# Expert groups: the one-hot block as stationary operand, four transposes after it, and the next one-hot block formed before the fourth expert's copy

## What is computed

```python
def hierarchical_moe(xn, w_group, w_router, w_gate, w_up, w_down):
    xt = xn.reshape(T, D)                                  # 256 x 1024, f32
    group_p = softmax(xt @ w_group)                        # 8 groups
    group_w, group_id = lax.top_k(group_p, 1)              # one group a token
    in_group = ...                                         # its 4 experts' logits
    top_logits, local_id = lax.top_k(in_group, 2)          # two of the four
    gates = group_w * softmax(top_logits)
    ...
    def expert_block(args):
        xb, e = args
        h = silu(xb @ w_gate[e]) * (xb @ w_up[e])          # 1024 -> 256
        return h @ w_down[e]                               # 256 -> 1024
    ...                                                    # y = sum of gate * expert output
```

## Time and profile before

| | us |
|---|---|
| median of 3 runs | 2758.59 |
| lowest, highest | 2754.98, 2763.64 |
| the profiled execution | 2754.4 |
| its span in the profile | 2752.6 |

### The profile page before, as it was taken

The page is one execution under the profiler, slowest core; times in us unless marked ns, Lnnn a source line. Parts: engine busy times, 40 slices in busy tenths (PEclk is TensorE's granted clock), DMA queues, the critical chain, the costliest instruction groups (busy, mean ns, idle before and its releaser), DMA issues. The chain is left out here.

```text
span 2752.6 us, 27889 instructions
## 1 busy us (share of the span) xinstructions
PE 2201.7 (80%) x8660; PEld 1182.1 (43%) x8660; DVE 1349.2 (49%) x2884; ACT 771.5 (28%) x2246; POOL 1050.1 (38%) x1107
## 2 busy tenths in 40 slices
PE   4778886766877878878877767769789998889997
PEld 2455552322333343434533222226555555655554
DVE  5656567865467466465664754441522223332222
ACT  1324232332434333353342333332410002410001
POOL 4015556667666546555566666650000000000000
PEclk9788988888998989989998988889889999978998
DMA  9548889999999999989999999992069994218995
GB/s 362 205 147 337 313 308 408 350 377 406 408 413 410 404 353 387 364 312 364 348 337 358 407 376 366 373 350 93 21 239 412 405 408 149 77 66 353 391 406 218
DMA packets 236993, 879.67 MB, mean 320 GB/s; under 512 B 23282, under 2 KB 29954, under 8 KB 214338
## 3 DMA queue, kind: packets, MB, share of 16 engines
q0 software_dynamic: 149488, 543.97, 51.6%
q1 hardware_dynamic: 87380, 334.23, 30.9%
HBM read 877.07 MB, written 1.05 MB: 319 GB/s over the span
## 5 line engine op out<-in xcount | busy, mean ns | idle before, releaser
L1481 PE MATMUL PS<-arena 128*128 128x512 f32 x2048 | 1032.4, 655 | 355.6 <-issue 197.1
L2117 DVE CUSTOM_DVE_ANT_0 JK<-arena,PS 128x1024 bf16<-128x1024 f32 x512 | 625.1, 1221 | 418.9 <-DMA arena<-in_peer_u_dram,IDX 293.1
L1481 PEld LDWEIGHTS PS<-arena 128*128 128x128 f32 x2048 | 407.3, 208 | 939.6 <-issue 889.9
L892 POOL DMA_INDIRECT arena<-in_peer_v_dram,IDX x512 | 500.2, 977 | 462.9 <-PE PS L1481 248.8
L889 POOL DMA_INDIRECT arena<-in_peer_u_dram,IDX x512 | 504.6, 986 | 334.7 <-DVE IDX L2090 162.7
L1031 ACT ACTIVATE ACTV<-DOT 128x1 f32<-128x1 f32 x512 | 102.0, 199 | 755.4 <-DVE DOT L2117 496.9
L1831 PE MATMUL PS<-arena,HT 128*64 128x256 f32 x2048 | 238.0, 385 | 0.0
L1044 ACT ACTIVATE arena<-IDENT,GACT 128x128 f32<-128x128 f32 x512 | 205.5, 401 | 91.3 <-remote 63.1
L1831 PEld LDWEIGHTS PS<-arena,HT 128*64 128x64 f32 x2048 | 142.6, 138 | 85.6 <-issue 21.4
L1039 ACT ACTIVATE GACT<-ACTV,GATE 128x1 f32<-128x1 f32 x512 | 150.8, 295 | 21.6 <-issue 3.5
L1459 PE MATMUL PS<-HT,arena 128*128 128x128 f32 x896 | 125.3, 304 | 35.3 <-issue 33.9
(11 more groups left out here) (339 smaller groups left out, 1863.8 us busy)
## 6 DMA issues: line engine op xcount, KB each, us to landing
arena<-in_w_gate_dram SPq DMA_DIRECT2D x64, 1024.0 KB, 9.5
arena<-in_w_up_dram SPq DMA_DIRECT2D x64, 1024.0 KB, 11.5
arena<-in_w_down_dram SPq DMA_DIRECT2D x64, 1024.0 KB, 8.2
arena<-in_w_ada_dram SPq DMA_DIRECT2D x24, 2048.0 KB, 12.3
arena<-in_w_in_dram SPq DMA_DIRECT2D x11, 2048.0 KB, 14.7
arena<-in_peer_wq_dram SPq DMA_DIRECT2D x10, 2048.0 KB, 8.1
arena<-in_w_out_dram SPq DMA_DIRECT2D x6, 2048.0 KB, 8.5
arena<-in_peer_u_dram,IDX POOLq DMA_INDIRECT x512
```

The source lines that it names most:

```text
L892: pool.indirect_dma_start(out=GV[b], out_offset=None, in_=v_rows, in_offset=off).then_inc(v_loaded[b], 16)
L1481: last = pe.matmul(PO[:, half, :], DIAG[:, n % DIAGS, :], GV[BUF[n]][:, half * 512:(half + 1) * 512], start=(j == 0), stop=False, skip_gro ...
L2117: dve.tensor_tensor_reduce(JUNK, GU[BUF[n]], HP[tt].rearrange("p b n -> p (b n)"), 1.0, 0.0, ALU.mult, ALU.add, DOT[:, s:s + 1]).then_inc( ...
```

## The change

`pick` swaps its operands. For each token tile and each half of the width, SEL's 64 slot columns (128x64) are stationary and 512 columns of HR move; the halves go to PSUM partitions 0 to 63 and 64 to 127 of bank 0. That is 4 matmuls in place of 16, and the result is not turned. ACT copies bank 0 (128x512) to a new buffer XS. A new step `turn_picked` transposes XS in four blocks of 128 columns into bank 1, and ACT copies that (128x512) to HTB, whose layout is now (m, c, t) with slice k = 4c + m. The semaphores rows_turned and rows_turned_out carry the two new hand-overs; picked and picked_out count one for each group, not two.

On PE turn_picked stands behind down of the group before and ahead of turn; slot_gates moves from behind the first gate and up to ahead of it, except in a layer's first group. On DVE, select of the next group stands ahead of the wait for the fourth expert's gate and up and of its copy, no longer behind them.

```diff
-        HTB = HTF[:, 0:KT * BT].rearrange("p (k t) -> p k t", k=KT)
+        HTB = HTF[:, 0:KT * BT].rearrange("p (m c t) -> p m c t", c=2, t=BT)
...
+        XS = mod[:, 9752:10264]
...
 # ACT, body, s == 0
-                        for c in range(2):
-                            act.wait_ge(picked, 2 * i + (2 * l * NGB + c + 1))
-                            act.activation(HTB[:, c * 4:(c + 1) * 4].rearrange("p k t -> p (k t)"), PS[:, c, 0:4 * BT],
-                                           ACT.Copy).then_inc(picked_out, 1)
+                        act.wait_ge(picked, i + (l * NGB + 1))
+                        act.activation(XS, PS[:, 0, :], ACT.Copy).then_inc(picked_out, 1)
+                        act.wait_ge(rows_turned, i + (l * NGB + 1))
+                        act.activation(HTB.rearrange("p m c t -> p (m c t)"), PS[:, 1, :], ACT.Copy).then_inc(rows_turned_out, 1)
...
 # PE
-                    for k in range(KT):
-                        for tt in range(TT):
-                            last = pe.matmul(PS[:, k // 4, (k % 4) * BT:(k % 4 + 1) * BT], HR[:, tt, k * P:(k + 1) * P],
-                                             SEL[:, tt, 0:BT], start=(tt == 0), stop=(tt == 1))
-                        if k % 4 == 3:
-                            last.then_inc(picked, 1)
+                    for tt in range(TT):
+                        for c in range(2):
+                            last = pe.matmul(PS[c * BT:(c + 1) * BT, 0, :], SEL[:, tt, 0:BT],
+                                             HR[:, tt, c * 512:(c + 1) * 512], start=(tt == 0), stop=(tt == 1))
+                    last.then_inc(picked, 1)
+
+                def turn_picked(i):
+                    pe.wait_ge(picked_out, i + (l * NGB + 1))
+                    for m in range(4):
+                        last = pe.transpose(PS[:, 1, m * P:(m + 1) * P], XS[:, m * P:(m + 1) * P], IDENT)
+                    last.then_inc(rows_turned, 1)
...
+                    if s == 0:
+                        turn_picked(i)
                     if n:
                         turn(*before(i, s, 1))
+                    if s == 0 and n:
+                        slot_gates(i)
...
+                    if s == 0:
+                        pe.wait_ge(rows_turned_out, i + (l * NGB + 1))
                     for k in range(KT):
-                        if s == 0 and k % 4 == 0:
-                            pe.wait_ge(picked_out, 2 * i + (2 * l * NGB + k // 4 + 1))
...
-                    if s == 0:
+                    if s == 0 and not n:
                         slot_gates(i)
...
 # DVE, body
-                    dve.wait_ge(gate_up_done, b + 1)
-                    if s == 0:
-                        dve.wait_ge(slot_gates_out, i + (l * NGB + 1))
-                    dve.tensor_scalar(GUO[:, s % 2], PS[:, 2 + s % 2, 0:DE], GS[:, s:s + 1], None,
-                                      ALU.mult).then_inc(gate_up_out, 1)
                     if s == EXP_RING - 1:
                         if n == EXP_RING:
                             dve.wait_ge(added, 2 * TT * i + 2 * TT * l * NGB)
                         dve.wait_ge(sel_turned, i + (l * NGB + 1))
                         dve.wait_ge(sel_step, i + (l * (NGB + 1) + 1))
                         select(i + 1)
+                    dve.wait_ge(gate_up_done, b + 1)
+                    if s == 0:
+                        dve.wait_ge(slot_gates_out, i + (l * NGB + 1))
+                    dve.tensor_scalar(GUO[:, s % 2], PS[:, 2 + s % 2, 0:DE], GS[:, s:s + 1], None,
+                                      ALU.mult).then_inc(gate_up_out, 1)
```

More of the change, by code:

```diff
@@ L583, in build @@
         gates_placed = sem("gates_placed")
+        rows_turned = sem("rows_turned")
+        rows_turned_out = sem("rows_turned_out")
         slot_gates_done = sem("slot_gates_done")
@@ L1296, in body @@
                         act.activation(SELT.rearrange("p t q -> p (t q)"), PS[:, 5, 0:TT * P], ACT.Copy).then_inc(sel_turned_out, 1)
-                blocks(act, l, body, silu, [(picked_out, *groups(l, 2)), (silu_done, *passes(l)),
+                blocks(act, l, body, silu, [(picked_out, *groups(l)), (rows_turned_out, *groups(l)), (silu_done, *passes(l)),
                                             (slot_gates_out, *groups(l)), (sel_turned_out, *groups(l))])
@@ L1826, in body @@
                         pe.wait_ge(expert_loaded[s], i * 48 + (l * NBX // EXP_RING + 1) * 48)
+                    if s == 0:
+                        pe.wait_ge(rows_turned_out, i + (l * NGB + 1))
                     for k in range(KT):
-                        if s == 0 and k % 4 == 0:
-                            pe.wait_ge(picked_out, 2 * i + (2 * l * NGB + k // 4 + 1))
                         for c, w in enumerate((WG[s], WU[s])):
-                            last = pe.matmul(PS[c * BT:(c + 1) * BT, 2 + s % 2, 0:DE], HTB[:, k, :],
+                            last = pe.matmul(PS[c * BT:(c + 1) * BT, 2 + s % 2, 0:DE], HTB[:, k % 4, k // 4, :],
                                              w[:, k, :], start=(k == 0), stop=(k == KT - 1))
                     last.then_inc(gate_up_done, 1)
-                    if s == 0:
+                    if s == 0 and not n:
                         slot_gates(i)
@@ L1842, in flush @@
                         spread_rows(i, tt, 2 * tt)
-                blocks(pe, l, body, flush, [(picked, *groups(l, 2)), (gate_up_done, *passes(l)), (turned, *passes(l)),
+                blocks(pe, l, body, flush, [(picked, *groups(l)), (rows_turned, *groups(l)), (gate_up_done, *passes(l)), (turned, *passes(l)),
                                             (down_done, *passes(l)), (slot_gates_done, *groups(l)),
```

## The result

| | us |
|---|---|
| before, median of 12 runs | 2767.24 (2754.92 to 2778.34) |
| changed, median of 12 runs | 2740.22 (2729.81 to 2756.17) |
| ratio, 95% interval | 0.9905 (0.9878 to 0.9931) |
| changed, profiled execution and its span | 2742.74, 2741.0 |

The change makes the kernel 27 us faster, 19 to 34 by the interval. The forecast was 34.6 us off a median of 2758.59, so 2724, with a range of 2713 to 2740: the direction is right, the gain four fifths of the forecast, and the time 0.2 us above the range. Three things were off. One decides the gain: a term of the sum, the spare time of the weights' loads.

What follows compares the result with a forecast made beforehand. PE was taken to bound the expert loops, with the DMA queue 0.69 us per group behind. Gains of 13.6 (layer 0), 14.1 (layer 1) and 6.4 us (clock drops), 34 in all, gave 2724 us, range 2713 to 2740.

Steps and rivals of the forecast that it cites:

- Select, 1.05: Between two groups, DVE's earlier select hides behind gate and up, so PE's wait before pick goes: 1.05 us gained per handover.
- Pick, 1.84: Pick as 4 wide matmuls of down's shape takes 1.87 us in place of 3.71: 1.84 us gained per handover.
- Four transposes, 0.87: The new transposes of the picked rows on PE cost 0.87 us per handover, between 0.74 and 1.04.
- Second copy, 0 with up to 0.3 kept: ACT's copy after the transposes hides behind turn and slot_gates: cost 0, with 0.3 us kept for the range.
- Sum of a handover, 2.0: Select plus pick minus transposes: 2.0 us gained per handover, range 1.6 to 2.3; 28.3 us over both layers.
- First group, 0: A layer's first group, without cover and mostly at 1.2 GHz: new pick, copies and transposes 6.98 us against 6.99, gain 0.
- Drops of the clock: Layer 1's two groups of 33.99 us, slowed by clock drops inside pick, return to normal: 6.4 us gained.
- Spare time of the loads: Weight loads have 5 to 10 us of spare, likeliest 8 to 10, while the queue falls behind 1.3 us per group.
- Loads bind early: Rival: loads bind from the first group, only the queue's dry moments, 9.7 us, are gained: 2743 to 2749 us; chance 0.08.
- Drops stay: Rival: the clock drops stay, two of them at other places, so 28 us are gained: 2731 us; chance 0.13.
- Halves apart: Rival: the new pick's two halves don't run side by side, a handover gains 0.4 us: 2747 us; chance 0.04.
- slower: Rival: six transposes and slot_gates in a row pull the clock down at every handover, 10 us slower: 2769 us; chance 0.04.

Runs made afterwards that it cites:

- split wait: Changed kernel with a semaphore of its own for down's weights, so gate and up waits only for its own two transfers: median 2611.16 us, ratio to before 0.9858.
- select_late: Changed kernel with select put back behind the fourth expert's copy, the new pick kept: loops 238.1 and 238.6 us, ratio to before 0.9898.
- select_early: Kernel before with only select moved ahead of the fourth expert's copy, pick still narrow: loops 242.8 and 243.2 us, ratio to before 0.9889.
- changed again: Changed kernel profiled once more with nothing edited, on another chip: loops 239.4 and 237.5 us, median 2613.66 us, ratio to before 0.9877.
- slot_gates behind: Changed kernel with slot_gates back behind the first gate and up: loops 237.9 and 237.5 us, one execution 2736.55 us.

## Why the prediction was right and wrong

- **PE bounds the loop, the queue stands 0.69 us behind it with 30.1 us a group.** Right: the queue's pace is 30.1 wherever it rules, and halving down's loads leaves the kernel before at 30.79.
- **Select, 1.05.** 1.10 in the changed kernel's row; alone 0.99, on top of the new pick 1.14. Right.
- **Pick, 1.84.** 3.71 became 1.72, so 1.99. The row of down was the right one. The rule of the Trainium skill's "TensorE: Matmul & The Clock Gate", Part 3 (Packing small matmuls), that weight loads overlap only between different row groups, does not hold for these halves: all eight loads are inside the 1.72.
- **Four transposes, 0.87.** They take 0.49, below the range's 0.74. This was a misreading. A transpose makes one record, not two as the other fp32 matmuls do, so the text ahead of the prediction is wrong that four make eight. The x8 of the earlier trace rows are eight transposes (the loop at L1348 has two halves of four blocks, and the three passes from 2440 to 2484 us have 24 records). The 64 turns of two have 128, from `--source`:

```profile
L1348 PE MATMUL PS<-IDENT,HR x24: 272/273/473, 2441.9 to 2471.1; 128*128 128x128 f32 x24
L1808 PE MATMUL PS<-IDENT,mod x128: 272/327/476, 2051.8 to 2735.4; 128*128 128x128 f32 x128
```

  Eight in 0.87 are 0.11 each, 0.44 for four, and the six of the changed kernel take 0.71 (2084.61 to 2085.32), 0.12 each. Read so, the sum of a handover would have been 2.45.
- **Second copy, 0 with up to 0.3 kept.** It costs 0.21, in the range.
- **Sum of a handover, 2.0.** It is 2.76 by the distance of the copies (30.79 to 28.03). By the rows of layer 0 (2.74) the transposes account for 0.38 of the difference; pick, turn and the first gate and up give 0.12 to 0.15 each, select and down 0.05 each, and the wait for the second copy with slot_gates takes 0.18 back.
- **First group, 0.** In layer 0 pick to gate and up takes 6.25 us (2052.82 to 2059.07) for 6.99, and gate and up to slot_gates 5.07 for 4.65. Together 0.3 us are gained; 0 was right within that, with luck: its 1.97 for four transposes at the low clock was again the row of eight (four take 1.11 there), and half of what this gained went into a longer gate and up.
- **Drops of the clock.** Both went, and 6.4 us with them; the granted clock is 1.00 in both loops behind the first group. In 42 handovers of the kernel before (three profiles, one with half of down's loads) there are 4 drops, in 84 with the new pick none. The base was not fair, though: this profile had two, the other two had one each.
- **Spare time of the loads: the step that failed.** The text took up's transfer of the fourth expert, 19.4 us from issue to use, as the shortest. But gate and up waits for a count of 48, gate, up and down. Down's transfer is issued last, at 2265.2, and was used at 2279.33, 14.1 us later, with a median of 7.7 to land: 6.4 us of spare, not 8 to 10. That spare, used by a PE that runs 0.7 us faster for each group than the sum had it, ran out in the third distance of layer 0 and the fourth of layer 1. A queue 2.07 us behind in each group is 14.5 us behind after seven, 8.1 more than the spare; 19.3 - 8.1 leaves 11.2, and layer 0 gained 10.8. The split wait shows the deadline, and halving down's loads shows the price: 8.9 and 7.4 us. The same wrong transfer gave the bound of 12.9 to 15.2; with down's, 2265.2 + 7.7 - 4.8 against 2279.33, it is 11.2 too. Once the loads bind, the gain of a layer is the dry moments and the spare, 4.8 + 6.4 us, however fast PE is, so the cheap transposes could not add to it. The terms were 13.6 and 14.1, the loops show 10.8 and 12.3 (18.7 with the two drops in the kernel before). That layer 1 could take its full 14.1 failed with it: the time that its long groups had given the queue went with the drops.
- **The base.** Loops of before with the mean of the three profiles' drops (1.33) against the changed ones give 29.5 - 0.67 x 3.2 = 27.4 us; the twelve runs on each side give 27.0. That this fits to 0.4 us is luck: in the other two sets of runs the medians gain 3 to 15 us more than the loops. The gain was forecast 7.6 us too high, some 4.6 of them from the spare time and 2.1 from drops that a median holds fewer of, the base 8.6 us too low, and both missed in the same direction for the absolute time, 16 us in all.
- **The rivals.** "Loads bind early" had the right mechanism with too high a price: it let the spare time count for nothing, 9.7 us where the loops show 23.1 without the drops. "Drops stay" is out, since none stayed in the loops, and "faster" by the median. "Halves apart" and "slower" are out: pick takes 1.72, and no handover of the changed kernel drops the clock, with six transposes and slot_gates (two matmuls of 4 columns, four records) in a row. What the Trainium skill says in Part 4 (PE-mode transpose) of the same page would have lowered it there; the granted clock stays at 1.00 in all 84 handovers.

Open: whether pick's narrow matmuls or the 0.92 us of standing still ahead of them brought the drops. With the wait and wide matmuls (select_late) there is no drop in 14 handovers, with narrow matmuls and no wait (select_early) none in 14 either; at 4 in 42 neither says much. Open too is where the 12 to 15 us beyond the loops come from in the set with select_early.

## What to carry to other kernels

When an engine gets faster next to a queue that is nearly full, work out how far the queue may fall behind, and do it for the transfer that the wait really asks for: read the count of the semaphore, since one wait for a whole set makes its last-issued transfer the deadline. Two improvements of the same engine then draw on one supply of spare time, so their single gains don't add up, and the second may be worth nothing. Before a profiled execution serves as base, cut it into stages and see which of them the change touches; those repeat within a microsecond here, apart from drops of the clock, while the whole moves by 23 us from run to run (12 runs of the kernel before) and by some 120 between sets of runs. Before a row serves as a price, count in the code how many operations its records are: here x8 meant eight transposes and was read as four.

## What was not expected of the hardware

- The same kernel took 2648 us on one chip and 2767 and 2777 in the other two sets of runs, 4.5 and 4.9% apart. In the profiles all of it is ahead of layer 0's first select, a stage that holds the gathers of single expert rows (1923 to 1932 against 2038 to 2061 us); which part of that stage it is, and whether the chip is the cause, no run shows. The expert groups took the same time on all of them.
- The queue's pace hardly varied: 30.1 us for 12.58 MB, 417 to 418 GB/s, in the four kernels' profiles in which it was the bound (changed, changed again, split wait, slot_gates behind), in all three sets of runs.
- Eight fp32 transposes in a row take 1.04 us at a granted clock of 1.00 (0.87 until the next matmul starts) and 1.97 at 0.50, in the mixer of the kernel before: the granted clock sets their pace too.
